# Rows of rounded tokens and of their rests: 1296 bytes apart instead of 1280, in a two-model float32 forward pass

## What is computed

```python
for i in range(DEPTH):
    hn = rmsnorm(h, norm_mix[i])
    h = h + mixer(hn, ...)
    h = h + swiglu(rmsnorm(h, norm_ffn[i]), w_in[i], w_out[i])
return rmsnorm(h, norm_final)[:, N_META:]
```

## Time and profile before

| | |
|---|---|
| time of three executions | 1358.15, 1358.15, 1358.73 us; median 1358.15 |
| span of the profiled execution, first to last instruction | 1356.6 us, some 1.6 us under the median time |
| TensorE matmul / weight load busy | 1350.0 / 1289.1 us |
| VectorE / ScalarE / GpSimd busy | 1010.7 / 709.1 / 295.4 us |
| moved by DMA | 229.72 MB, 169 GB/s over the span |

### The profile page before, as it was taken

How to read it: one execution, slowest core, us unless ns; L and a number is a source line. 1 busy time by engine, 2 the same in 40 slices (tenths; PEclk the granted TensorE clock), 3 DMA queues, 4 the chain that set the end, 5 groups by cost and what they waited for, 6 DMA issues and landing times.

```text
span 1356.6 us, 24729 instructions
## 1 busy us (share of the span) xinstructions
PE 1350.0 (100%) x9873; PEld 1289.1 (95%) x9873; DVE 1010.7 (75%) x1613; ACT 709.1 (52%) x1167; POOL 295.4 (22%) x313
## 2 busy tenths in 40 slices
PE   9999999999999999999999999999999999999998
PEld 9999999999999888899999999999999999988886
DVE  6788766656987988778877876766557885898843
ACT  7565544434756555544444664544435565655543
POOL 1136000023152000132355744000023533120000
PEclk9999999999999999999999999999999999999999
DMA  8334665665443655565543455555554553566552
GB/s 279 125 125 158 191 192 185 190 186 162 136 157 126 214 190 194 170 197 181 163 134 125 155 186 158 185 174 171 170 172 150 183 161 121 172 199 189 189 184 77
DMA packets 220457, 229.72 MB, mean 169 GB/s; under 512 B 13664, under 2 KB 207704, under 8 KB 220344
## 3 DMA queue, kind: packets, MB, share of 16 engines
q1 hardware_dynamic: 219232, 226.24, 52.1%
q10 hardware_dynamic: 1112, 1.90, 0.6%
HBM read 226.80 MB, written 1.33 MB: 168 GB/s over the span
## 4 chain that ended last, share of the span: by engine, by line
PE 99%; DMA 0%; issue 0%; DVE 0%; ACT 0%; ACTq 0%; DVEq 0%
PE ps L591 28%; PE ps L589 21%; PE ps L590 20%; PE ps L586 8%; PE ps L584 6%; PE ps L1148 2%; PE ps L1147 2%; PE ps L1146 1%; PE ps L650 1%; PE ps L649 1%; PE ps L651 1%; PE ps L917 1%; PE ps L787 1%; PE ps L992 1%; PE ps L775 0%; PE ps L1080 0%
## 5 line engine op out<-in xcount | busy, mean ns | idle before, releaser
L1188 ACT ACTIVATE uh<-raw 128x1024 fp32r<-128x1024 f32 (+4 forms) x452 | 446.8, 999 | 441.4 <-PE ps L591 380.5
L1785 DVE TENSOR_TENSOR ul<-raw,uh 128x1024 fp32r<-128x1024 f32 (+3 forms) x448 | 529.8, 1190 | 132.7 <-PE ps L591 84.6
L591 PE MATMUL ps<-xx,ul 128*128 128x272 f32 (+1 forms) x2136 | 609.3, 285 | 0.0
L589 PE MATMUL ps<-xx,uh 128*128 128x272 f32 (+1 forms) x1448 | 422.8, 292 | 0.0
L590 PE MATMUL ps<-xx,uh 128*128 128x272 f32 (+1 forms) x1448 | 413.8, 286 | 0.0
L591 PEld LDWEIGHTS ps<-xx,ul 128*128 128x128 f32 x2136 | 401.3, 188 | 0.0
L589 PEld LDWEIGHTS ps<-xx,uh 128*128 128x128 f32 x1448 | 272.3, 188 | 3.0 <-issue 1.7
L590 PEld LDWEIGHTS ps<-xx,uh 128*128 128x128 f32 x1448 | 272.6, 188 | 0.8
L591 PE MATMUL ps<-aa,ul 128*128 128x272 f32 (+1 forms) x920 | 260.6, 283 | 0.0
L589 PE MATMUL ps<-aa,uh 128*128 128x272 f32 (+1 forms) x788 | 228.6, 290 | 0.0
L590 PE MATMUL ps<-aa,uh 128*128 128x272 f32 (+1 forms) x788 | 226.7, 288 | 0.0
(11 more groups left out here) (345 smaller groups left out, 1706.5 us busy)
## 6 DMA issues: line engine op xcount, KB each, us to landing
raw<-in_ffn_w SPq DMA_DIRECT2D x62, 1024.0 KB, 5.3
raw<-in_ffn_w_in SPq DMA_DIRECT2D x44, 1024.0 KB, 5.2
raw<-in_ret_w_in SPq DMA_DIRECT2D x24, 1024.0 KB, 5.1
raw<-in_ffn_w_out SPq DMA_DIRECT2D x16, 1024.0 KB, 5.6
raw<-in_gla_w_in SPq DMA_DIRECT2D x11, 1024.0 KB, 5.1
raw<-in_ret_w_o SPq DMA_DIRECT2D x8, 1024.0 KB, 5.2
raw<-in_dsa_w_in SPq DMA_DIRECT2D x7, 1024.0 KB, 5.6
raw<-in_ffn_w_out SPq DMA_DIRECT2D x8, 768.0 KB, 4.9
```

The lines of the kernel that those rows point to most:

```text
L589: e.matmul(ps[:, 0:n1 - n0], hi[:, k, :], x.hi[:, k0 + j, n0:n1], start=first and j == 0, stop=False)
L591: i = e.matmul(ps[:, 0:n1 - n0], lo[:, k, :], jh[k0 + j] if x.joined else x.hi[:, k0 + j, n0:n1], start=False, stop=last and j == len(ks) - 1)
L1188: i = e.activation(unit_hi(u)[:, :, cols], a, ACT.Copy)
L1785: i = e.tensor_tensor(unit_lo(u)[:, :, cols], a, unit_hi(u)[:, :, cols].bitcast(F32), ALU.subtract)
```

## The change

One constant. A row of 272 columns is followed by the next 324 elements, 1296 bytes, further on.

```diff
-ROW = 320
+ROW = 324
```

## The result

The changed kernel takes 1363.56 us (median of five runs, 1363.26 to 1363.76) against 1358.36 us (five runs, 1358.15 to 1358.73): ratio 1.0038, 95% interval 1.0025 to 1.0050. It is slower by 5.2 us; 1363 was forecast.

A forecast was written before the change was run, and what follows sets the result against it. TensorE, never idle, was taken as the bound through distances between matmul starts. Terms summed to +4.2 us, a rhythm estimate gave +5.3; +4.8 on 1356.6 gave 1361.4, plus 1.55 to the median: 1363 us, 8-in-10 range 1345 to 1384.

The forecast's parts named there:

- Step 1: 272-column steps of `xx`, 1304 steps: tokens and rests at one distance make each 2.3 ns dearer, +3.0 us, bounds ±8.7 us.
- Step 2: 272-column steps of `aa`, 672 steps: no change, bounds ±4.5 us.
- Step 3: 256-column steps go to a middle price: 144 of `xx` get cheaper, −0.5 us; 244 of `aa` dearer, +0.8 us.
- Step 4: Line 586: 352 steps on `xx` get 4.6 ns dearer, +1.6 us; 132 on `aa` stay, 0.
- Step 5: Line 584, 352 steps: each goes to a middle price, 2.1 ns cheaper, −0.7 us.
- Step 6: The last product, 88 steps: no change, bounds ±0.6 us.
- The second way: Some 3200 steps: each row starting 16 bytes on in the 64-byte rhythm costs 1.67 ns, +5.3 us in all.
- The signs it named: Changed timeline: 272-column `xx` steps at 375 to 376 ns, period 4 or 16 rows; line 586 near 351, 584 near 349.
- One more piece of 64 bytes: Rival: reads beginning inside a 64-byte piece touch another, 6.67 ns each; 1404 us, or 1370 to 1385 partly hidden; chance 0.17.
- The short wait: Rival: last rhythm cut by 12 columns, −5.0 ns on 3200 steps, 1342 us; weaker form 1352 us; chance 0.28.
- No difference at all: Rival: losses are averages over any row distance, so the new average equals the old; 1358 us, chance 0.25.
- PE and ACT never wait on anyone: Skill's sentence; with its 16-byte cachelines, the prediction read it as 16-byte row steps costing nothing, sum 0.

## Why the prediction was right, and where its steps were not

- **What bounds the kernel, and that nothing but the distances between starts would move**: right. The waits, the clock and the other engines stayed, and the kinds of steps make up all of the 5.2 us. That 1363 met 1363.56 is in good part luck all the same: two causes behind it are wrong, and errors of both signs lie in its terms.
- **Step 1, 272 columns of `xx`**: right in size (+3.6 us for +3.0), wrong in its cause. It put the loss on tokens and rests at one distance, and took the price from lines 586 and 584 as if only the place told them apart; with line 584's parts put at the places of 586 its step went to 353.4 ns and not to 346.7. That distance does have a price, 6.3 ns a step and not 2.3, while rows do not drift; with drift alone, and tokens and rests still 128 apart, the kind lost 2.6 of its 3.6 us. Halving 4.6 ns between two rows gave the right number by chance.
- **Step 2, `aa`**: the claim that it would not react failed; +1.1 us in the changed kernel and +1.4 with drift alone. The earlier trace rows compare two places that happen to cost the same, and the prediction took that for a sign that place hardly counts for 272 columns. The weights at 0 bring the same steps to 380.0 ns.
- **Step 3**: the dearer 256-column steps of `xx` fell as said (-0.6 for -0.5); those of `aa` hardly rose (+0.2 for +0.8).
- **Step 4**: sign right, price halved: line 586 went up by 2.1 ns and not by 4.6. **Step 5**: line 584 gained 0.3 ns and not 2.1. That both now stand at 350 to 351 ns looks like averaging over places, but for line 584 it is not: at fixed places it pays 351.1 or 353.2 ns, and with drift by 64 bytes 348.3. **Step 6**, the last product: +0.3 us for 0, within its bounds.
- **The second way, 1.67 ns for each step**, falls: rows that drift by 64 bytes lose as much, and there no 16 bytes need to be waited for. Its sum was wrong as well: of 16 equally likely waits 12 would lose 1.67 ns and 4 gain 5.0, which is 0 on average, and it charged 1.67 ns to all 3200 steps. The 0.6 us that it added to the forecast have nothing behind them.
- **The signs it named**: 272-column steps of `xx` dearer and uneven, line 586 at 350 ns and `xx` and `aa` moving the same way came out; the period is eight rows, where it said 4 or 16, and line 584 stayed at 351 where it said 349.
- **The rivals.** One more piece of 64 bytes (1404 us) is excluded by the changed kernel itself and by the kernel moved by 16 bytes. The short wait (1342 us) is excluded: in the changed kernel only the 256-column steps of `xx` fell clearly, by some 4 ns, and they are 144 of 3200. No difference at all is excluded by the interval from 1.0025 on, but its reason has something in it: the kernel before stood under the mean of the fixed prices in its most frequent kind (373.7 against 375.2 ns). That drifting rows pay that mean is not what the traces show.
- **The rule "PE and ACT never wait on anyone"** (the Trainium skill, SBUF — State Buffer, "Who interferes with whom"): for other engines this case's trace agrees: the steps are 373.3 ns both in the earlier trace rows, where VectorE is busy 15.4 and ScalarE 11.1 of 23.5 us, and in the earlier trace rows, where they are busy 10.3 and 7.1. The sentence is about engines that wait for one another. The prediction stretched it to the place of TensorE's own operands, and to that it does not reach: 64 bytes between weights and tokens are worth up to 6.2 ns a step of 272 columns.

## What to carry to other kernels

Where TensorE is never idle, read the start-to-start distance of matmuls by kind of step in the timeline, and compare kinds with equal columns: a difference between them can be a price of layout, which a constant changes. It need not be: line 584's could not be had by moving its parts, so only a run tells. A fixed, well chosen place for all rows was 0.3% better here than rows that drift, but a badly chosen fixed place was worse than both. An experiment that takes a change of layout apart has to even out the lengths of the tiles, or it moves everything behind them too.

## What was not expected of the hardware

- At 2.4 GHz, three matmuls of 272 columns in `float32r` with a load each take 373.3 ns and not 340. The steady stretches with fixed places repeat in whole multiples of 6.67 ns, over one to six steps.
- One set of places can run at two prices, 373.4 and 380.0 ns or 346.7 and 353.3, for tens of steps each, and the price changed where other matmuls came between two steps. What makes the loss of some 10% and what chooses between the two stays open.
- 16 bytes between weights and tokens have no effect beyond 0.1 us over the whole kernel; 64 bytes have one of 7.2 us one way (1365.77 us) and 2.4 the other (1360.83).
- Rows that change place from one to the next do not pay the mean of the prices of those places: 375.9 ns for a mean of 374.2, and 348.3 where the places cost 351.1 and 353.2.
- Parts of a change do not add up: 128 bytes on the rests of `xx` cost 8.6 us alone and, together with the other moves, under 1 us once the rows drift.
